# A two-block transformer on one core: residual, its projections and the norms turned from feature-major to token-major

## The chip, the core and the metric

The kernel runs on one core of a Trainium2 chip. TensorE (PE) multiplies; VectorE (DVE) and ScalarE (ACT) do elementwise work; GpSimd (POOL) does some; SyncE (SP) issues the DMAs. Every engine runs its own instruction stream in order, and semaphores order them among each other. The metric is the device time of one execution in microseconds.

## The reference

256 tokens of width 1024 pass through two blocks, everything in float32. Cut to what matters:

```python
def rmsnorm(x, g):
    return x * lax.rsqrt(jnp.mean(x * x, -1, keepdims=True) + EPS) * g

# block 1
u = rmsnorm(x, norm_mix_g);  p = u @ w_in + b_in          # q, kv, hq, hf, hi, hg, ga, gb
ya = window_attention(p) @ w_branch_attn;  yb = hgrn2(p) @ w_branch_hgrn
h = x + (sigmoid(ga) * ya + sigmoid(gb) * yb) @ w_out
u = rmsnorm(h, norm_ffn_g)
h = h + (silu(u @ w_ffn_gate) * (u @ w_ffn_up)) @ w_ffn_down      # hidden width 2816
x = rmsnorm(h, norm_final_g)
# block 2, modulated by a vector c
sh_m, sc_m, g_m, sh_f, sc_f, g_f = split(silu(c) @ w_ada + b_ada, 6)
h = rmsnorm(x, norm_mix_w) * (1 + sc_m) + sh_m
x = x + g_m * (concat(ssd(h @ w_in_2), chunk_attention(h @ w_in_2)) @ w_out_2)
h = rmsnorm(x, norm_ffn_w) * (1 + sc_f) + sh_f
x = x + g_f * (conv_ffn(h, w_up, w_down))
return rmsnorm(x, final_norm_w)
```

## The kernel before

All matrix products are float32 done as three fp32r products: a value is split into a high part (H) and a low remainder (L), and PE adds H·H, L·H and H·L. A weight matrix streams through in *panels* of four blocks of 128 rows by 512 columns (1 MB). SP loads a panel into one of 4 slots of `raw`; ACT writes its high part `wH` (L611, `split_hi`), DVE the remainder `wL` (L881 for the name `wL`, `split_lo`), both into one of 3 slots. The split of panel q+2 stands in the streams of ACT and DVE where PE starts panel q, so PE has two panels of cover. The operand of the products is `p1H`/`p1L`, `pyH`/`pyL` or `zH`/`zL`, [feature, k, token].

The order of all this is written out in `timeline()`: a list of events (panel, evac, tail, norm, ...), and every engine walks the same list and issues its own part of each event. Nothing is reordered.

Most groups (`GROUPS`, 512 output columns) are `cm`, feature-major: 128 weight columns are stationary and 256 tokens move (L1340, 128x256), four tiles to a group. `hi0`, `hi1`, `v2` and part of `kv` are `tm`, token-major: 128 tokens are stationary and the weight columns move (L1343, 128x512), two tiles to a group. The projections back to the residual are `out0`, `out1` (8 blocks each), `down0`, `down1` (22 blocks), `oo0`, `oo1` (8), `dd0`, `dd1` (22), all `cm`, and each tile is added on DVE to the residual `hT` [feature, k, token].

Norm n: 0 before `q0`, 1 before the gated FFN `f0`..`f10`, 2 before `xs`, 3 before `u0`, 4 at the end. ACT squares `hT` (L615), PE sums over the features by a matmul against `ones` (L1402; L1312 for norm 2), ACT takes the root (L634), DVE the reciprocal (L908), PE spreads it over the partitions (L1306), DVE scales (L884), ACT writes `p1H` (L642, L645), DVE `p1L`. At the start PE turns x with 16 transposes (L1302) while ACT squares the loaded rows.

The modulation `silu(c) @ w_ada` is a sum over rows on DVE: 24 panels of `w_ada` (event `ada`, four operations on `acc` each), and after every second one PE sums over the partitions (event `ada_sum`, L1438) and DVE reads the four columns into `mod`. `WITH_ADA` says with which weight panels they come: `q0`, `q1`, `ga1`, `out0`, `out1`, each `f`, and four each in `down0` and `down1`.

Of the kernel before, what the change touches and what calls it, by code (L numbers as in the profile page):

```python
# [5 lines left out]
F32 = mybir.dt.float32  # L6
# [7 lines left out]
P = 128  # L14
D = 1024
# [32 lines left out]
def tm_tiles(off, width):  # L48
    return [("tm", 2 + j, off, width, j) for j in range(TB)]
# [8 lines left out]
for _i in range(2):  # L58
# [5 lines left out]
    GROUPS[f"out{_i}"] = group("w_out", [(_i * W, W)], cm_tiles(4 - 4 * _i), "DDDD", "P1")  # L64
    GROUPS[f"down{_i}"] = group("w_ffn_down", [(_i * W, W)], cm_tiles(), "DDDD", "Z", KF)
    GROUPS[f"oo{_i}"] = group("w_out_2", [(_i * W, W)], cm_tiles(), "DDDD", "PY")
    GROUPS[f"dd{_i}"] = group("w_down_2", [(_i * W, W)], cm_tiles(4 - 4 * _i), "DDDD", "Z", KF)
# [16 lines left out]
WITH_ADA = [(_n, 1) for _n in ("q0", "q1")] + [("ga1", 0)]  # L84
WITH_ADA += [(_n, 0) for _n in ("out0", "out1")] + [(f"f{_i}", 0) for _i in range(NF)]
WITH_ADA += [(_n, _i) for _n in ("down0", "down1") for _i in range(4)]

# [5 lines left out]
def timeline():  # L93

    tl = [("load_x",), ("norm", 0), ("vectors",)]
# [3 lines left out]
    def gemm(name, *after):  # L99

        parts = len(GROUPS[name]["parts"])
        for i in range(parts):
# [3 lines left out]
            if (name, i) in WITH_ADA:  # L106
                j = next(ada)
                tl.append(("ada", j))
                if j % 2:
                    later.append(("ada_sum", j // 2))  # L110
# [4 lines left out]
            if i < len(after):  # L115
                tl.extend(after[i])

# [26 lines left out]
    gemm("out1", [("squares", 1)], [("norm", 1)])  # L144
    for i in range(NF):
        gemm(f"f{i}")
    gemm("down0")
    gemm("down1", [], [], [("squares", 2)], [("first_sums",)], [("mod",)], [("norm", 2)])
    assert next(ada, None) is None, "every panel of w_ada has its place"
    gemm("xs", [("h_final",)])  # L150
    gemm("bc", [("dt",)])
    gemm("q2", [], [("xdt",), ("sA", 0)])
# [4 lines left out]
    gemm("oo1", [("squares", 3)], [("norm", 3)])  # L157
    for i in range(NF):
        gemm(f"u{i}")
    gemm("dd0")  # L160
    gemm("dd1", [("gain",)], [("turn",)], [("squares", 4)], [], [], [("norm", 4), ("store",)])
# [3 lines left out]
def build(nc, IN, out):  # L165
# [17 lines left out]
    with ExitStack() as ctx:  # L183
# [8 lines left out]
        on.bcast = ctx.enter_context(nc.semaphore("bcast"))  # L192
# [69 lines left out]
        on.ot_done = ctx.enter_context(nc.semaphore("ot_done"))  # L262
        on.ot_psum = ctx.enter_context(nc.semaphore("ot_psum"))
# [12 lines left out]
        on.ms2_done = ctx.enter_context(nc.semaphore("ms2_done"))  # L276
        on.rt2_done = ctx.enter_context(nc.semaphore("rt2_done"))
        on.rd2_done = ctx.enter_context(nc.semaphore("rd2_done"))
# [28 lines left out]
        on.x_done = ctx.enter_context(nc.semaphore("x_done"))  # L307
        on.x_psum = ctx.enter_context(nc.semaphore("x_psum"))
# [3 lines left out]
        on.xr_zero = ctx.enter_context(nc.semaphore("xr_zero"))  # L312
        on.yT_done = ctx.enter_context(nc.semaphore("yT_done"))
# [48 lines left out]
        hT = sb("hT", [P, KD, T])  # L362
# [39 lines left out]
        OT, OUT = scr(28, KD, T), scr(8, TB, D)  # L402
# [1276 lines left out]
```

## Time and profile before

| | |
|---|---|
| time, median of 3 runs | 903.29 us (903.15 to 903.71) |
| span of the profiled execution | 902.7 us; the page gives no other time for it |
| PE busy | 859.8 us, 95% |
| DVE busy | 579.5 us, 64% |
| ACT busy | 474.3 us, 53% |
| POOL busy | 29.8 us, 3% |
| DMA queue q1 | 158.15 MB, 53.2% of 16 engines |
| mean granted clock of PE | 0.973 |

A row of the timeline is one instruction or a run of equal ones: start and duration in microseconds from the start of the span, engine, line of the kernel, operation, output<-inputs and shape, and in brackets how long the engine had been idle and what ended that. PE's durations overlap, since matmuls are pipelined: what a matmul costs a full PE is the distance to the next start, here called its pitch. PE's clock has two levels, granted 1.0 (2.4 GHz) and 0.5 (1.2 GHz).

### The profile page before, as it was taken

The numbers are of one execution on the slowest core, as the hardware profiler recorded it, in microseconds if no ns is written. First come the engines' busy times: TensorE is split into PE (matmuls) and PEld (weight loads), VectorE is DVE, ScalarE is ACT, GpSimd is POOL, SyncE is SP. The second block draws the span as 40 slices with busy tenths as digits, with TensorE's granted clock in tenths as the row PEclk, the third lists the DMA queues.
The fourth block names the chain that finished last, engine by engine and source line by source line (L and its number), as shares of the span: only waits on it lengthen the run. The fifth ranks groups of instructions, "written<-read, shape, count | busy, mean of one in ns | idle before, by whom it ended". The sixth has DMA issues, their size and how long they took to land. (4 is left out here: it accounts for less than half of the span.)

```text
span 902.7 us, 16064 instructions
## 1 busy us (share of the span) xinstructions
PE 859.8 (95%) x6874; PEld 841.7 (93%) x6874; DVE 579.5 (64%) x764; ACT 474.3 (53%) x687; POOL 29.8 (3%) x52
## 2 busy tenths in 40 slices
PE   5999999999899999999999999998989999999997
PEld 4999989999899989999999998997879999999997
DVE  5655457546646877777777767675444778777452
ACT  6656787637533444344333335735444666666342
POOL 3000001000100010000000000000001000000010
PEclk9999999999999989999999998999989999999999
DMA  9645344425442677888877864442424355654521
GB/s 315 237 154 189 124 140 141 154 81 187 143 138 79 206 229 245 267 258 260 266 256 274 278 230 174 153 141 63 144 66 149 97 184 187 187 187 164 188 71 47
DMA packets 105400, 159.18 MB, mean 176 GB/s; under 512 B 4320, under 2 KB 52720, under 8 KB 105328
## 3 DMA queue, kind: packets, MB, share of 16 engines
q1 hardware_dynamic: 105328, 158.15, 53.2%
q8 instruction: 54, 0.88, 0.4%
q14 instruction: 18, 0.15, 0.0%
HBM read 157.07 MB, written 1.06 MB: 175 GB/s over the span
## 5 line engine op out<-in xcount | busy, mean ns | idle before, releaser
L1340 PE MATMUL ps<-p1H,wH 128*128 128x256 f32 x1320 | 382.0, 289 | 10.6 <-DVE wL L881 4.6
L881 DVE TENSOR_TENSOR wL<-raw,wH 128x2048 fp32r<-128x2048 f32 (+1 forms) x126 | 282.4, 2243 | 154.6 <-ACT wH L611 154.0
L1340 PE MATMUL ps<-p1L,wH 128*128 128x256 f32 x1320 | 378.2, 286 | 0.0
L1340 PE MATMUL ps<-p1H,wL 128*128 128x256 f32 x1320 | 377.9, 286 | 0.0
L611 ACT ACTIVATE wH<-raw 128x2048 fp32r<-128x2048 f32 (+1 forms) x126 | 235.5, 1870 | 181.2 <-PE ps L1340 179.1
L1340 PEld LDWEIGHTS ps<-p1H,wH 128*128 128x128 f32 x1320 | 258.5, 196 | 12.0 <-DVE wL L881 4.9
L1340 PEld LDWEIGHTS ps<-p1L,wH 128*128 128x128 f32 x1320 | 258.6, 196 | 0.1
L1340 PEld LDWEIGHTS ps<-p1H,wL 128*128 128x128 f32 x1320 | 258.1, 196 | 0.0
L1340 PE MATMUL ps<-zH,wH 128*128 128x256 f32 x352 | 100.2, 285 | 2.2 <-DVE arena L881 1.1
L1340 PE MATMUL ps<-zL,wH 128*128 128x256 f32 x352 | 99.6, 283 | 0.0
L1340 PE MATMUL ps<-zH,wL 128*128 128x256 f32 x352 | 99.6, 283 | 0.0
L1340 PEld LDWEIGHTS ps<-zH,wH 128*128 128x128 f32 x352 | 67.5, 192 | 2.4 <-DVE wL L881 1.2
L1340 PEld LDWEIGHTS ps<-zL,wH 128*128 128x128 f32 x352 | 67.5, 192 | 0.0
L1340 PEld LDWEIGHTS ps<-zH,wL 128*128 128x128 f32 x352 | 67.5, 192 | 0.0
L884 DVE SCALAR_TENSOR_TENSOR acc<-raw,cact,acc 128x512 f32<-128x512 f32 x84 | 63.8, 759 | 2.6
L1340 PE MATMUL ps<-pyH,wH 128*128 128x256 f32 x192 | 55.8, 290 | 2.0 <-DVE pyL L881 1.2
L884 DVE SCALAR_TENSOR_TENSOR arena<-arena,par 128x256 f32<-128x256 f32 x120 | 50.0, 481 | 11.7 <-ACT arena L720 9.0
L1340 PE MATMUL ps<-pyL,wH 128*128 128x256 f32 x192 | 54.9, 286 | 0.0
L1340 PE MATMUL ps<-pyH,wL 128*128 128x256 f32 x192 | 54.8, 285 | 0.0
L659 ACT ACTIVATE arena<-ps 128x256 f32<-128x256 f32 x82 | 29.5, 377 | 26.7 <-PE ps L1340 26.3
L1340 PEld LDWEIGHTS ps<-pyH,wH 128*128 128x128 f32 x192 | 37.4, 195 | 2.7 <-issue 2.6
L1340 PEld LDWEIGHTS ps<-pyL,wH 128*128 128x128 f32 x192 | 37.5, 195 | 0.0
(247 smaller groups left out, 921.2 us busy)
## 6 DMA issues: line engine op xcount, KB each, us to landing
raw<-in_w_in SPq DMA_DIRECT2D x40, 1024.0 KB, 5.5
raw<-in_w_ada SPq DMA_DIRECT2D x24, 1024.0 KB, 5.2
raw<-in_w_up SPq DMA_DIRECT2D x44, 512.0 KB, 4.6
raw<-in_w_ffn_gate SPq DMA_DIRECT2D x22, 512.0 KB, 4.0
raw<-in_w_ffn_up SPq DMA_DIRECT2D x22, 512.0 KB, 5.4
raw<-in_w_ffn_down SPq DMA_DIRECT2D x10, 1024.0 KB, 5.5
raw<-in_w_down SPq DMA_DIRECT2D x10, 1024.0 KB, 5.0
raw<-in_w_out SPq DMA_DIRECT2D x8, 1024.0 KB, 5.1
```

What stands on the lines that cost most here:

```text
L611: nc.scalar.activation(wH[:, q % NHL, 0:nk, 0:wd], raw[:, i % NRAW, 0:nk, 0:wd], ACT.Copy).then_inc(on.w_hi, 1)
L659: nc.scalar.activation(dst(m), ps[:, t[1], 0:T], f, **bias).then_inc(on.evac_act, 1)
L881: return v.tensor_tensor(o, a, b, op)
L884: return v.scalar_tensor_tensor(out=o, in0=a, scalar=s, in1=b, op0=op0, op1=op1)
L1340: last = mm(ps[:, t[1], 0:T], wt[:, slot, k, t[2]:t[2] + P], at_[:, k0 + k, :], start=st, stop=en)
```

## The change

- The residual is `res` [token, feature], loaded straight into place; PE no longer turns x.
- `out`, `down`, `oo`, `dd` become `tm` groups of two tiles (j = 0, 1: the token halves), in other banks. In `group`, the odd two blocks of `down` and `dd` come first.
- The squares are summed by ACT itself (`accum_out`) over rows of 512; what the first half of the features gives is put together early (`before`). Root and reciprocal are taken for each token half (`root`, `turn_over`), and for j = 0 of `out1`, `oo1`, `dd1` inside the evacuation of the group, ahead of tile 1.
- The rows are scaled into `UN`, j = 0 by POOL (`scale`), j = 1 by DVE, 256 features at a time, and PE turns them back in four pieces of four transposes: two ahead of the first product, one after its block 1, one after block 2. ACT and DVE then write `p1H`, `p1L` from PSUM.
- The gates g_m and g_f are needed along rows: POOL writes a diagonal form `DG`, two float32 matmuls of 128x512 against `ones` spread it, ACT copies it (event `gate`, after the first panel of `q2` and of `u0`).
- The `ada` panels go to `ga0`, `hq0`, `hq1`, `hf1`, `bh0`, `out0` (2), `out1`, `f0`..`f9`, `down0` (5), `down1` (1), into buffers of their own, and PE's sums are gathered: 4 at norm 1, 2 at the end of `f10`, 4 at norm 2, 2 at norm 3.
- The final gain comes as a broadcast row by DMA; there are four output DMAs of 256 KB in place of two.

```diff
 def group(weights, segments, tiles, evac, operand, kblocks=KD, kbase=0):
-    parts = [(k, min(KP, kblocks - k)) for k in range(0, kblocks, KP)]
+    head = kblocks % KP
+    parts = [(0, head)] * (head > 0) + [(k, KP) for k in range(head, kblocks, KP)]
...
+    GROUPS[f"out{_i}"] = group("w_out", [(_i * W, W)], tm_tiles(0, W, 4 - 2 * _i), "DD", "P1")
+    GROUPS[f"down{_i}"] = group("w_ffn_down", [(_i * W, W)], tm_tiles(0, W, 4 - 2 * _i), "DD", "Z", KF)
+    GROUPS[f"oo{_i}"] = group("w_out_2", [(_i * W, W)], tm_tiles(0, W, 2 - 2 * _i), "DD", "PY")
+    GROUPS[f"dd{_i}"] = group("w_down_2", [(_i * W, W)], tm_tiles(0, W, 4 - 2 * _i), "DD", "Z", KF)
...
-WITH_ADA = [(_n, 1) for _n in ("q0", "q1")] + [("ga1", 0)]
...
+WITH_ADA = [(_n, 0) for _n in ("ga0", "hq0", "hq1", "hf1", "bh0", "out0")] + [("out0", 1), ("out1", 0)]
+WITH_ADA += [(f"f{_i}", 0) for _i in range(10)]
+WITH_ADA += [("down0", _i) for _i in range(1, 6)] + [("down1", 0)]
+
+ADA_READ = {1: (0, 4), "down0": (4, 2), 2: (6, 4), 3: (10, 2)}
...
-    gemm("oo1", [("squares", 3)], [("norm", 3)])
-    for i in range(NF):
+    gemm("oo1", [("squares", 3)], sums(3) + [("norm", 3)])
+    gemm("u0", [("gate", 1)])
+    for i in range(1, NF):
...
+            def scale(n):
+
+                pool.wait_ge(on.rd_done, 2 * n + 1)
+                for c in range(4):
+                    pool.tensor_scalar(UN[:, 0, wide(c)], (Y if n == 2 else res)[:, 0, wide(c)], R1[:, 0:1], None,
+                                       ALU.mult).then_inc(on.us0, 1)
...
+                elif e[0] == "gate":
+                    g = e[1]
+                    pool.wait_ge(on.ada_done, (2, 4)[g])
+                    pool.wait_ge(on.u_ready, (24, 32)[g])
...
+            def turn_over(n, j):
...
+                dve.wait_ge(on.rt_done, 2 * n + j + 1)
+                v.reciprocal(R1[:, j:j + 1], R0[:, j:j + 1]).then_inc(on.rd_done, 1)
...
+                        dve.wait_ge(on.tile_done, TILE[name, j])
+                        if n < 3:
+                            tt(hb, o, hb, ALU.add).then_inc(on.evac_dve, 1)
+                        else:
...
+                            step(tt(gt, o, gates[n - 3][:, half(i)], ALU.mult))
+                            tt(hb, gt, hb, ALU.add).then_inc(on.evac_dve, 1)
...
+                        if i == 1 and j == 0 and n != 2:
+                            turn_over(n, 0)
...
+            def turn(n, c):
+
+                pe.wait_ge(on.us0, 4 * n + c + 1)
+                pe.wait_ge(on.us1, 4 * n + c + 1)
+                if c > 1:
+                    pe.wait_ge(on.u_ready, 8 * n + 2 * c - 2)
+                for k in (2 * c, 2 * c + 1):
+                    for j in range(TB):
+                        last = tr(un(k)[:, j * P:(j + 1) * P], UN[:, j, k * P:(k + 1) * P])
+                last.then_inc(on.ut_psum, 1)
...
                     for k in range(nk):
                         pe.wait_ge(*operand_ready(name, k))
                         for t in g["tiles"]:
                             last = product(t, k)
+                        if name in NORM_OF and 0 < k < 3:
+                            turn(NORM_OF[name], k + 1)
```

The names below are those of the program: `arena` is the SBUF area that holds `UN`, `DG`, `TMP` and others, `R` the roots and reciprocals. ACT at the start of the program, before and then in the change (waits in brackets):

```order
L634 ACTIVATE R<-XSS,eps 128x2 [waits ss_done]
L611 ACTIVATE wH<-raw 128x2048 [waits raw0]
L642 ACTIVATE p1H<-arena 128x256 [waits tmp_done] x8
L611 ACTIVATE wH<-raw 128x2048 [waits raw1]
L752 ACT_TABLE_LOAD
```

```order
L679 ACTIVATE R<-XS,pre 128x1 [waits sq_done,pre_done]
L650 ACTIVATE wH<-raw 128x2048 [waits raw0]
L702 ACTIVATE p1H<-ps,par 128x256 [waits ut_psum] x8
L650 ACTIVATE wH<-raw 128x2048 [waits raw1]
L814 ACT_TABLE_LOAD
```

The high part of the second panel (raw1) still follows all eight `p1H`, which now wait for PE's transposes.

PE at norm 1, between the last product of `out1` and the first of `f0`, before and then in the change:

```order
L1340 MATMUL ps<-p1H,wL 128x256
L1402 MATMUL ps<-ones,arena 128x1 x10
L1306 MATMUL ps<-ident,R 128x128 x2
L1340 MATMUL ps<-p1H,wH 128x256
```

```order
L1431 MATMUL ps<-wL,p1H 128x512
L1489 MATMUL ps<-ones,acc 128x1 x8
L1489 MATMUL ps<-ones,arena 128x1 x8
L1396 MATMUL ps<-ident,arena 128x128 x8
L1428 MATMUL ps<-p1H,wH 128x256
```

The sums of squares and the spread are gone; four of the modulation's sums and eight transposes stand there.

POOL from norm 1 to norm 3, before and then in the change:

```order
L594 TENSOR_TENSOR arena<-arena 128x256 [waits sq_done]
L594 TENSOR_TENSOR arena<-arena 128x256 [waits sq_done,pool_step] x2
L588 MEMSET arena 128x2048 [waits u_ready]
```

```order
L574 TENSOR_SCALAR arena<-arena,R 128x256 [waits rd_done]
L574 TENSOR_SCALAR arena<-arena,R 128x256 x3
L629 MEMSET arena 128x2048 [waits h_final,u_ready]
L635 TENSOR_TENSOR arena<-ident,mod 128x1024 [waits u_ready,ada_done]
L574 TENSOR_SCALAR arena<-res,R 128x256 [waits rd_done]
L574 TENSOR_SCALAR arena<-res,R 128x256 x3
L635 TENSOR_TENSOR arena<-ident,mod 128x1024 [waits u_ready,ada_done]
```

L635 writes `DG`. The second one waits until all eight `p1L` of norm 3 stand (`u_ready`), and PE's spread of the gate stands behind the first panel of `u0`.

## Rows read from the trace of the kernel before

**Rows 1.** The chain that ended last: start us, us, what.

```profile
701.03 171.45 PE ps L1340 x1416
872.47 0.87 PE ps L1302 x8
```

**Rows 2.** Timeline of PE at the token-major group hi0 and what follows it.

```profile
215.60 0.40 PE L1343 MATMUL ps<-wH,p1H 128*128 128x512 f32 x1
...
226.51 0.28 PE L1340 MATMUL ps<-p1H,wH 128*128 128x256 f32 x1
```

**Rows 3.** Timeline, the last of twelve modulation sums on PE.

```profile
535.26 0.95 PE L1438 MATMUL ps<-ones,acc 128*128 128x1 f32 x8
...
536.07 0.36 PE L1340 MATMUL ps<-zH,wH 128*128 128x256 f32 x1
```

**Rows 4.** Timeline, banks that down0 and then down1 wait for.

```profile
469.03 0.36 PE L1340 MATMUL ps<-zH,wH 128*128 128x256 f32 x1 [1.15 <-DVE arena L881]
...
503.75 0.36 PE L1340 MATMUL ps<-zH,wH 128*128 128x256 f32 x1 [1.06 <-DVE hT L881]
```

**Rows 5.** Timeline of the start, PE, ACT and DVE.

```profile
16.51 0.58 PE L1340 MATMUL ps<-p1H,wH 128*128 128x256 f32 x1 [4.62 <-DVE wL L881]
...
19.38 1.90 ACT L611 ACTIVATE wH<-raw 128x2048 fp32r<-128x2048 f32 x1
...
25.84 3.70 ACT L611 ACTIVATE wH<-raw 128x2048 fp32r<-128x2048 f32 x2
...
27.77 4.49 DVE L881 TENSOR_TENSOR wL<-raw,wH 128x2048 fp32r<-128x2048 f32 x2 [4.17 <-ACT wH L611]
```

**Rows 6.** Timeline around norm 1.

```profile
324.88 2.29 DVE L881 TENSOR_TENSOR wL<-raw,wH 128x2048 fp32r<-128x2048 f32 x1 [0.29 <-ACT wH L611]
...
328.24 0.28 PE L1340 MATMUL ps<-p1H,wL 128*128 128x256 f32 x1
...
333.49 0.55 PE L1340 MATMUL ps<-p1H,wH 128*128 128x256 f32 x1 [1.57 <-DVE p1L L881]
```

**Rows 7.** Groups by line and shape: busy, mean ns | idle before, releaser.

```profile
L881 DVE TENSOR_TENSOR arena<-ps,brow 128x512 f32<-128x512 f32 x4 | 2.6, 680 | 0.0
L826 ACT ACTIVATE arena<-ps 128x512 f32<-128x512 f32 x4 | 2.4, 592 | 0.0
L1044 DVE TENSOR_SCALAR arena<-hT,par 128x256 f32<-128x256 f32 x8 | 2.4, 344 | 0.0
```

**Rows 8.** Timeline at norm 2 and norm 3.

```profile
538.90 0.28 PE L1340 MATMUL ps<-zH,wL 128*128 128x256 f32 x1
...
546.67 0.55 PE L1340 MATMUL ps<-p1H,wH 128*128 128x256 f32 x1 [0.87 <-DVE p1L L884]
...
695.63 0.28 PE L1340 MATMUL ps<-pyH,wL 128*128 128x256 f32 x1
...
698.08 0.26 ACT L634 ACTIVATE R<-ps,eps 128x2 f32<-128x2 f32 x1 [1.19 <-PE ps L1402]
...
701.03 0.55 PE L1340 MATMUL ps<-p1H,wH 128*128 128x256 f32 x1 [1.72 <-DVE p1L L884]
```

**Rows 9.** Stretch behind norm 3: length, busy PE, PEld, DVE, ACT, POOL, clock, DMA.

```profile
701.03:704.00 2.97, 2.97 (x14) 2.97 (x15) 2.97 (x9) 1.92 (x4) 0.00 (x0) 0.51 0.03 6
```

**Rows 10.** The chain: one float32 matmul of 128x256, in two instructions.

```profile
636.29 0.43 PE ps L1468 x2
```

**Rows 11.** Timeline, GpSimd.

```profile
8.63 0.37 POOL L564 TENSOR_SCALAR M<-CL 128x64 f32<-128x64 f32 x1
...
154.96 2.41 POOL L577 TENSOR_TENSOR arena<-arena 128x1024 f32<-128x1024 f32 x1 [143.32 <-ACT arena L810]
```

**Rows 12.** Instructions on acc: duration ns min/median/max.

```profile
L1098 DVE TENSOR_SCALAR acc<-raw,cact x12: 478/480/960, 32.2 to 522.2; 128x512 f32<-128x512 f32 x12
```

**Rows 13.** Timeline of the end.

```profile
893.22 0.28 PE L1340 MATMUL ps<-zH,wL 128*128 128x256 f32 x1
...
897.44 1.41 DVE L1076 TENSOR_SCALAR arena<-ps,R 128x512 f32<-128x512 f32 x2
```

More of the change, by code:

```diff
@@ L80 @@
 NU1 = 6
-WITH_ADA = [(_n, 1) for _n in ("q0", "q1")] + [("ga1", 0)]
-WITH_ADA += [(_n, 0) for _n in ("out0", "out1")] + [(f"f{_i}", 0) for _i in range(NF)]
-WITH_ADA += [(_n, _i) for _n in ("down0", "down1") for _i in range(4)]
+WITH_ADA = [(_n, 0) for _n in ("ga0", "hq0", "hq1", "hf1", "bh0", "out0")] + [("out0", 1), ("out1", 0)]
+WITH_ADA += [(f"f{_i}", 0) for _i in range(10)]
+WITH_ADA += [("down0", _i) for _i in range(1, 6)] + [("down1", 0)]
+ADA_READ = {1: (0, 4), "down0": (4, 2), 2: (6, 4), 3: (10, 2)}
+READS = list(ADA_READ)
+NORM_OF = {"q0": 0, "f0": 1, "xs": 2, "u0": 3}
+RES = {1: "out", 2: "down", 3: "oo", 4: "dd"}
 class Signals:
@@ L116, in gemm, with sums @@
                 tl.extend(after[i])
+    def sums(n):
+        q, count = ADA_READ[n]
+        return [("ada_sum", q + i, n) for i in range(count)]
     def X(u):
@@ L143, in timeline @@
     gemm("out0")
-    gemm("out1", [("squares", 1)], [("norm", 1)])
-    for i in range(NF):
+    gemm("out1", [("squares", 1)], sums(1) + [("norm", 1)])
+    for i in range(NF - 1):
         gemm(f"f{i}")
[L147 to L150, printed above, removed]
+    gemm(f"f{NF - 1}", [], sums("down0"))
+    gemm("down0", [("ada_read", "down0")])
+    gemm("down1", [], [], [("squares", 2)], [("mod", 0)], [], sums(2) + [("norm", 2)])
+    gemm("xs", [("h_final",), ("mod", 1)])
     gemm("bc", [("dt",)])
-    gemm("q2", [], [("xdt",), ("sA", 0)])
+    gemm("q2", [("gate", 0)], [("xdt",), ("sA", 0)])
     gemm("k2", [("sY", 0), ("sA", 1)], [("sY", 1), ("scores", 6)])
@@ L156, in timeline @@
     gemm("oo0", [("pt", 8), ("yT", 7), ("pv", 8), ("yT", 8)])
-    gemm("oo1", [("squares", 3)], [("norm", 3)])
-    for i in range(NF):
+    gemm("oo1", [("squares", 3)], sums(3) + [("norm", 3)])
+    gemm("u0", [("gate", 1)])
+    for i in range(1, NF):
         gemm(f"u{i}")
     gemm("dd0")
-    gemm("dd1", [("gain",)], [("turn",)], [("squares", 4)], [], [], [("norm", 4), ("store",)])
+    gemm("dd1", [], [], [("squares", 4)], [], [], [("norm", 4), ("store",)])
+    assert next(ada, None) is None, "every panel of w_ada has its place"
     return tl
@@ L633, in norm @@
-                sums = {0: XSS[:], 2: S12[:, :, 0], 4: ssf}.get(n, ss)
-                nc.scalar.activation(R0[:], sums, ACT.Sqrt, scale=1.0 / D, bias=eps[:, 0:1]).then_inc(on.rt_done, 1)
+                    for j in range(TB):
+                        square(0, 0, j)
+                for j in range(TB):
+                    square(n, 1, j)
+                    if n != 2:
+                        root(n, j)
                 if n == 4:
                     return
+                if n == 2:
+                    for j in range(TB):
+                        root(n, j)
@@ L761, in _ @@
                 elif k == "squares":
-                    for kk in range(4):
-                        square(e[1], kk)
+                    for j in range(TB):
+                        square(e[1], 0, j)
+                elif k == "gate":
+                    g = e[1]
+                    act.wait_ge(on.gate_psum, g + 1)
+                    if g == 0:
+                        act.wait_ge(on.conv_done, 24)
+                    for i in range(2):
+                        nc.scalar.activation(gates[g][:, half(i)], ps[:, 4 + i, :], ACT.Copy).then_inc(on.gate_done, 1)
                 elif k == "norm":
@@ L913, in norm @@
                     return
-                dve.wait_ge(on.bcast, n + 1)
+                dve.wait_ge(on.rd_done, 2 * n + 2)
+                for c in range(4):
+                    v.tensor_scalar(UN[:, 1, wide(c)], (Y if n == 2 else res)[:, 1, wide(c)], R1[:, 1:2], None,
+                                    ALU.mult).then_inc(on.us1, 1)
+                if n in ADA_READ:
+                    read_ada(n)
+                if n == 0:
+                    split_lo(0)
                 def low(k):
@@ L1437, in _ @@
                     for t in range(4):
[L1438 removed]
+                        o = 4 * (q - ADA_READ[n][0]) + t
+                        last = mm(adaps[n][:, o:o + 1], ACC[q][:, t * P:(t + 1) * P], ones[:, 0:1], start=True,
+                                  stop=True)
                     last.then_inc(on.ada_psum, 1)
[L1440 removed]
                 elif k == "scores":
```

450 lines of the change are left out of this document (211 added, 239 removed).

## The prediction, on record before the change was run

> **What bounds the kernel now.** I read the chain of waits first. From 701.03 PE issues 1416 matmuls of 128x256 in 171.45 us without a pause [rows 1]. That is most of block 2, and the page's 95% for PE says the same of the whole. So a microsecond is won where PE has less to issue, or where it stands still: at the start (first product at 16.51 [rows 5]), at norms 1, 2 and 3 (last product to next: 328.24 to 333.49 [rows 6]; 538.90 to 546.67 and 695.63 to 701.03 [rows 8]), at the end (893.22 to the span's 902.7 [rows 13]) and at two bank waits of 1.15 and 1.06 us [rows 4]. DVE and ACT have slack everywhere else. After a standstill comes a second cost: behind norm 3 the granted clock is 0.51, its lower level of 1.2 GHz, and 14 matmuls take 2.97 us [rows 9], 0.212 each against 0.120 for the others: (171.45 - 2.97) / 1402. Rows of the trace are taken against its span, 902.65 us; the median of the runs is 0.64 above it, and I add that at the end.
>
> **Wider products.** 48 matmuls of 128x512 run from 215.60 to 226.51 [rows 2], 0.2273 us each. Two of 128x256 cost 0.2404. The groups out, oo (64 products each), down, dd (176 each) make 480 x 3 = 1440 narrow matmuls, which become 720 wide ones: 720 x 0.0131 = **-9.4 us**. The pitch is that of the same form in the same kernel, so this term is firm.
>
> A rule speaks against it. The Trainium skill, "TensorE: Matmul & The Clock Gate", section "Wait — 56ns, not 53.3ns?", gives a full clock's pitch as columns / 2.4 GHz plus about 2.5 ns; by it halving the matmuls would save 2.5 ns for each of 720, an estimate of 1.8 us, and the sum would be 7.6 us higher. The rows show 13 ns, and they decide.
>
> **Modulation sums.** One lot (8 instructions on PE) stands between 535.26 and 536.07 [rows 3], 0.81 us, and there are 12 in line: 9.7 us. In the change ten of them stand in the waits of norms 1, 2 and 3, where PE has nothing else; the two behind f10 stay in line. Gain 10 x 0.81 = **-8.1 us**. If that cover were gone (the norms no longer wait), they would cost what they did. DVE's own part, about 3.1 us for each of 24 panels, only moves. In down0 and down1 it now stands in six panels in a row: 2.3 for a split and 3.1 together 5.4 us, against 24 x 0.227 = 5.45 on PE. PE's cover is two panels, so I take nothing and keep it as a rival. The sums of squares in down1 (16 instructions on PE, at 0.10 each as in [rows 3]) go: **-1.6 us**. The eight output transposes go from 872.47 [rows 1]: **-0.9 us**.
>
> **Bank waits.** Both [rows 4] end on DVE: down0 waits for the banks of f10, whose DVE step stood behind a read of the modulation; down1 waits for those of down0. In the change down0 writes banks 4, 5 and down1 banks 2, 3, and the read is behind: **-2.2 us**.
>
> **Norm 1.** Time is counted from the end of issue of the last product, E. DVE's split of the panel two ahead ends 327.17 (324.88 + 2.29), 1.2 us before E [rows 6], and about 0.9 before it now that the panel is shorter. Then in DVE's order: tile 0 (a 128x512 add with PSUM, 0.68 [rows 7]) to -0.2; ACT's square 0.59 plus the read of the accumulator, root 0.26 [rows 8], DVE's reciprocal, ready at +0.9. DVE has waited for it in `turn_over`, ahead of tile 1. Tile 1 to 1.6, square to 2.4, root and reciprocal to 2.95, first scaled piece to 3.3, all four by about 4.15. PE does four modulation sums to 3.3, the transposes from 3.4 (0.87 for eight [rows 1], more at the low clock), ACT's `p1H` to 4.8, DVE's `p1L` to 5.3. Before it was 5.13. With POOL in DVE's way (below) I take +0.5. Eight transposes more now stand inside the first panel: +0.9. Sum **+1.4**.
>
> **Norm 2.** Before 7.65. Now tile 0 and its gained copy `Y` to +0.5, tile 1 and its copy to 1.9, four squares on ACT to 2.65, two roots and two reciprocals one after the other to 3.95, four pieces to 5.1, TMP, `p1H`, `p1L` 1.4 more: 6.6. This is the norm where POOL's pieces fall on DVE's most; I take 7.85. With the transposes **+1.1**.
>
> **Norm 3.** Each tile now costs DVE two operations of 0.68 (gate, add). Tile 0 -0.95 to +0.45, its root and reciprocal to 1.7 with DVE waiting, tile 1 to 3.1, square, root, reciprocal to 4.4, pieces to 5.6, modulation read, TMP, `p1H`, `p1L` to 7.15, with POOL 7.5. Before 5.2: +2.3, transposes +0.9, **+3.2**. The clock's dip behind each norm I leave as it is.
>
> **The gates.** A float32 matmul of 128x256 takes 0.43 [rows 10], so one of 128x512 0.86; four of them in line **+3.4**. The first gate is ready long before. The second is not: POOL may write `DG` only when `p1L` 7 stands. With P the start of u0's first product: blocks 0 and 1 take to P+4.2 (2.97 us of it at the low clock), transposes to 4.6, block 2 to 6.05, transposes to 6.5, `p1L` 7 at 8.4, POOL's 128x1024 of 2.41 [rows 11] or more to about 11.2. PE has finished the panel at 7.95 and stands for **+3.3**. Another dip of the clock behind that is likely, 1.7 for a dip as long as at norm 3 (half of 3.4 us): **+1.7**.
>
> **The start.** Before: first product 16.51, high part of panel 1 from 19.38, then three table loads, high part of panel 2 from 25.84, its remainder done at 30.0; q1 began just then [rows 5]. The change frees DVE of the copies and lets the first product start near 15.3. But `p1H` 4 to 7 need transposes that stand behind blocks 1 and 2 of q0's first panel. At the low clock these blocks take until 20.4, so `p1H` 7 is ready at 23.7, and ACT's high part of panel 1 comes behind it: 23.7 to 25.6, remainder to 27.9, against a need at 24.3. The table loads follow: high part of panel 2 at 30.1, remainder 34.3, and q1 starts at 34.3 where it was 30.0, or at 35.4 if the clock dips in the standstill of 3.6. **+5.0**, between +4.2 and +6.
>
> **The end.** E to 902.7 is 9.3 us. In the change tile 1 runs to 1.6, root and reciprocal to 2.9, scaling to 4.0 where it was done 5.5 after E (897.44 + 1.41 [rows 13]); four DMA issues in place of two take back some: **-1.3**.
>
> **Sum.** -9.4 -8.1 -1.6 -0.9 -2.2 +1.4 +1.1 +3.2 +3.4 +3.3 +1.7 +5.0 -1.3 = -4.4: 898.3 of span, 898.9 as a median. POOL's scaling of 128x256 is in no row; it lies between 0.37 (64 columns) and 2.41 (two inputs, 1024) [rows 11]; I take 0.8.
>
> **Rivals.**
> - *The two new standstills don't come.* If the first products run at the full clock, or POOL's `DG` is done in time, the start (5.0) and the second gate (5.0) cost half or nothing: 891 to 895. For it: PE's order leaves one block's slack. Against it: the order of ACT and of POOL is fixed, and both chains are long. 894.
> - *DVE and POOL hold each other up.* An operation on `acc` of 0.48 us once took 0.96, while POOL was adding [rows 12]. If DVE's four pieces each wait for a piece of POOL's (0.8), norms 1 to 3 lose up to 1, 2.4 and 1, some 2.9 more than I took: 902. The Trainium skill, "SBUF — State Buffer", section "Who interferes with whom", says that DVE's `tensor_scalar` from SBUF to SBUF and a GpSimd operation exclude each other for a whole instruction; by that rule this rival is the forecast's neighbour, and the doubled duration agrees with it.
> - *Slower: DVE falls behind in down0.* Six panels at 5.4 us of DVE against 5.45 leave nothing for f10's tail (1.4) and down0's evacuation (4 x 0.68). And the loads are two of 1 MB in 5.45 us, 385 GB/s, over what q1 moves when it is full: 158.15 MB in 53.2% of 903 us, 329 GB/s. Twelve loads take 38 us where PE takes 30. It decides once the lag passes PE's cover, about 6.5 us; with 8 us of lag or DVE's and DMA's together, PE stands 4 to 8 us in down0 or down1, plus a clock dip: 906. Against it: four panels of `w_ada` in a row already ran here with no such wait in PE's list.
> - *The wide products save as little as the page's rule*: 906.
>
> **Chances.** Forecast 0.50, no standstills 0.17, DVE and POOL 0.14, slower 0.15, wide products 0.04. What a measurement of this kernel tells from no change is 0.2%, 1.8 us: faster means below 901.5, slower above 905.1. Faster: nine tenths of the forecast, the first rival, a third of the second: 0.66, which I cut to 0.64; slower: most of the last two, 0.17; between them 0.19. The range from 892 to 906 leaves out the lower end of the first rival and the upper end of the third.
>
> **What would show it.** Right: PE's pitch of 0.227 in out, down, oo and dd; no PE wait at the starts of down0 and down1; a standstill of 3 to 4 us ahead of q0's second panel, ended by `wL`; one of about 3 ahead of the gate's matmuls in u0, ended by POOL; gaps at norms 1, 2, 3 near 5.6, 7.9 and 7.5. Wrong: a PE wait on `wL` in down0 or down1; a dip of the clock that goes or comes where I left it; POOL's pieces far from 0.8.

## The result and the profile after

The changed kernel takes 909.92 us (median of 20 runs, 905.54 to 914.19), the kernel before 903.45 in as many. The ratio is 1.0064, 95% interval 1.0041 to 1.0086: slower by 0.6%, where 0.5% faster was forecast. The time lies above the forecast's range. The profiled execution has a span of 907.4 us, 4.7 more than the 902.7 of before; the forecast for it was 4.4 less.

The table sets the two traces side by side, stage by stage. A stage runs from the start of its first product to that of the next one's; the norms run from the end of issue of the last product to the first product, as in the prediction. The forecast's column puts its terms where they belong.

| stage | before | after | change | forecast |
|---|---|---|---|---|
| to the first product | 16.51 | 15.78 | -0.7 | -1.2 |
| q0 to attention | 35.22 | 40.58 | +5.4 | +5.4 |
| attention's first product to ba0 | 190.82 | 190.96 | +0.1 | 0 |
| ba0 to bh1 | 61.90 | 64.71 | +2.8 | 0 |
| out0, out1 | 23.91 | 21.79 | -2.1 | -2.1 |
| norm 1 | 5.13 | 8.64 | +3.5 | +0.5 |
| f0 to f10 | 135.54 | 131.83 | -3.7 | -3.5 |
| down0, down1 | 69.99 | 59.97 | -10.0 | -9.4 |
| norm 2 | 7.65 | 7.39 | -0.3 | +0.2 |
| block 2 up to oo0 | 118.25 | 123.62 | +5.4 | +2.6 |
| oo0, oo1 | 30.83 | 29.96 | -0.9 | -1.3 |
| norm 3 | 5.28 | 7.77 | +2.5 | +2.3 |
| u0 to u10 | 128.08 | 136.65 | +8.6 | +7.6 |
| dd0, dd1 | 64.23 | 59.87 | -4.4 | -4.4 |
| end | 9.36 | 7.88 | -1.5 | -1.3 |

Eleven of fifteen stages came within 0.6 us. Four carry the miss: ba0 to bh1 (2.8), norm 1 (3.0), block 2 (2.8) and u (1.0), together 9.6 us; span and forecast differ by 9.1, and the others give the rest back.

What was forecast as a new standstill is there. At the start, PE's timeline, then ACT's:

```profile
27.62 0.39 PE L1428 MATMUL ps<-p1H,wH 128*128 128x256 f32 x1 [3.63 <-DVE wL L950]
```

```profile
22.60 0.84 ACT L702 ACTIVATE p1H<-ps,par 128x256 fp32r<-128x256 f32 x2 [1.03 <-PE ps L1396]
23.32 1.91 ACT L650 ACTIVATE wH<-raw 128x2048 fp32r<-128x2048 f32 x1
25.25 1.28 ACT L814 ACT_TABLE_LOAD   x1
...
29.80 3.70 ACT L650 ACTIVATE wH<-raw 128x2048 fp32r<-128x2048 f32 x2
```

PE stands 3.63 us (forecast 3.6) for the split of panel 1, which ACT begins at 23.32, behind p1H 7 (forecast 23.7); the next split is at 29.80, where it was at 25.84 [rows 5]. In u0 PE stands for GpSimd's diagonals, as forecast (3.3), and then works at the low clock:

```profile
712.65 0.44 DVE p1L L950
713.20 1.94 POOLq L193
715.18 3.68 PE ps L1468 x4
```

These are pieces of the chain that ended last (start, us, what); PE's own row has [2.95 <-POOL arena L635] at 715.18.

**What was not forecast, first: DVE's order.** DVE's timeline ahead of bh1 and at norm 1:

```profile
294.80 0.48 DVE L1192 TENSOR_SCALAR arena<-raw,cact 128x512 f32<-128x512 f32 x1
295.32 2.33 DVE L953 SCALAR_TENSOR_TENSOR arena<-raw,cact,arena 128x512 f32<-128x512 f32 x3
297.68 2.29 DVE L950 TENSOR_TENSOR wL<-raw,wH 128x2048 fp32r<-128x2048 f32 x1
299.89 0.42 DVE L950 TENSOR_TENSOR arena<-ps,arena 128x256 f32<-128x256 f32 x1
...
330.08 3.11 DVE L953 SCALAR_TENSOR_TENSOR arena<-raw,cact,arena 128x512 f32<-128x512 f32 x4
333.23 0.17 DVE L972 TENSOR_SCALAR pre<-XS 128x2 f32<-128x2 f32 x1
333.30 2.28 DVE L950 TENSOR_TENSOR wL<-raw,wH 128x2048 fp32r<-128x2048 f32 x1
335.50 0.68 DVE L950 TENSOR_TENSOR res<-ps,res 128x512 f32<-128x512 f32 x1
337.36 0.16 DVE L981 RECIPROCAL R<-R 128x1 f32<-128x1 f32 x1 [1.18 <-ACT R L679]
337.44 0.67 DVE L950 TENSOR_TENSOR res<-ps,res 128x512 f32<-128x512 f32 x1
```

A panel of the modulation is read in 2.9 to 3.1 us. Before, none was read in the groups ba and bh. Now the panel that belongs to bh0 stands at 294.80, ahead of a split and of the evacuation of bh0's banks (299.89), and PE waits 1.59 us at 300.45, bh1's first product, for the first of these. At norm 1 the panel of out1 holds DVE until 333.19; the split ends at 335.58, 1.76 us after the end of PE's last product (333.82), where the forecast had it 0.9 ahead, and tile 0's add, which was to be done 0.2 ahead, starts at 335.50. Then tile 1's add waits for the root of tile 0, as forecast (337.36, 337.44). PE's own timeline at the two places:

```profile
300.45 0.36 PE L1428 MATMUL ps<-pyH,wH 128*128 128x256 f32 x1 [1.59 <-DVE arena L950]
...
335.52 2.83 PE L1489 MATMUL ps<-ones,arena 128*128 128x1 f32 x16
340.20 1.94 PE L1396 MATMUL ps<-ident,arena 128*128 128x128 f32 x8 [1.84 <-DVE arena L1000]
```

The four gathered sums end at 338.35 and PE then stands 1.84 us for DVE's scaled rows, so the sums themselves are not what makes norm 1 long.

**Second: the clock.** Windows of both traces (columns: us, length, then busy PE, PEld, DVE, ACT, POOL, the granted clock, DMA share, GB/s), before and after:

```profile
277.30:280.70 3.40, 2.94 (x14) 2.94 (x14) 0.20 (x1) 0.17 (x1) 0.00 (x0) 0.50 0.41 158
331.90:338.70 6.80, 5.23 (x25) 5.24 (x25) 5.99 (x16) 4.50 (x9) 0.00 (x0) 0.50 0.06 17
570.80:574.30 3.50, 3.50 (x18) 3.50 (x18) 1.05 (x6) 2.47 (x4) 0.00 (x0) 0.51 0.66 252
656.20:663.00 6.80, 6.25 (x23) 5.16 (x23) 3.16 (x9) 1.88 (x5) 0.00 (x0) 0.50 0.02 5
700.50:703.90 3.40, 2.87 (x13) 2.90 (x14) 3.40 (x9) 2.18 (x5) 0.00 (x0) 0.50 0.02 5
```

```profile
281.00:289.00 8.00, 6.66 (x34) 6.58 (x34) 3.67 (x6) 1.24 (x2) 0.00 (x0) 0.57 0.31 119
336.00:347.00 11.00, 8.83 (x44) 8.40 (x45) 4.85 (x13) 3.71 (x10) 3.66 (x4) 0.53 0.62 201
565.00:572.00 7.00, 7.00 (x35) 7.00 (x35) 3.60 (x8) 5.69 (x6) 0.00 (x0) 0.51 0.71 251
653.00:664.00 11.00, 9.38 (x34) 7.87 (x34) 4.64 (x14) 3.30 (x9) 0.00 (x0) 0.53 0.19 63
698.00:709.00 11.00, 7.94 (x38) 7.60 (x39) 5.21 (x15) 2.68 (x7) 2.90 (x3) 0.53 0.09 32
715.00:719.00 4.00, 3.82 (x7) 1.82 (x8) 2.27 (x1) 0.11 (x1) 0.12 (x1) 0.57 0.10 15
```

A window of 11 us at a mean of 0.53 holds 10.3 us at the low level of 1.2 GHz (11 x 0.47 / 0.5). So the low stretch at norm 1 grew from 6.8 to 10.3 us, that at norm 3 from 3.4 to 10.3, that at the y norm (653) from 6.8 to 10.3; those at 281 and 565 doubled, and those at 29 and 715 are new. Over the span the mean clock fell from 0.973 to 0.958: 902.7 x 0.027 / 0.5 = 49 us at the low level became 907.4 x 0.042 / 0.5 = 76. The forecast had added 3.4 for u0, and a dip at the start as a chance (q1 at 35.4 in place of 34.3).

Not all of the 27 us cost time. About 10 of them lie in the waits of the norms and at the end: the stretch at norm 1 runs from 336.3 to 346.6, the norm until 342.46, so that 4.1 us of it fall on f0, where it was 5.2 before (333.5 to 338.7). What costs is the low level where PE has products: by the ends of the stretches 3.4 us more at the start (29), 3.4 more at ba1 and bh0, 6 more in block 2, 6 more in u (5.4 behind norm 3 where it was 2.9, and 3.4 at 715). Block 2 as a whole, from the first product of xs to that of oo0, before and after:

```profile
546.67:664.92 118.25, 111.58 (x823) 105.57 (x823) 72.62 (x117) 62.73 (x102) 1.81 (x1) 0.94 0.40 134
```

```profile
541.65:665.27 123.62, 116.95 (x834) 109.68 (x835) 72.64 (x114) 63.47 (x105) 3.91 (x2) 0.92 0.39 128
```

In block 2 the narrow products of dt and those of the y norm fell into such stretches: from 561.2 to 567.8 where they took from 565.6 to 571.0 (1.2 us more), and from 654.07 to oo0 11.2 us instead of 9.7.

### The profile page after: what moved, and what is told of

It reads as the page before. It is cut to its first block and busy times, and to the rows that moved or that the text cites. A ratio compares the mean times of both kernels' runs of the same rounds, so it can differ in the third digit from the quotient of the medians.

```text
span 907.4 us, 14521 instructions
## 1 busy us (share of the span) xinstructions
PE 852.8 (94%) x6082; PEld 803.5 (89%) x6082; DVE 582.8 (64%) x742; ACT 479.0 (53%) x696; POOL 38.6 (4%) x60
## 5 line engine op out<-in xcount | busy, mean ns | idle before, releaser
L1431 PE MATMUL ps<-wH,zH 128*128 128x512 f32 x176 | 68.6, 390 | 0.0
L1431 PE MATMUL ps<-wL,zH 128*128 128x512 f32 x176 | 68.5, 389 | 0.0
L1431 PE MATMUL ps<-wH,zL 128*128 128x512 f32 x176 | 68.5, 389 | 0.0
L1396 PE MATMUL ps<-ident,arena 128*128 128x128 f32 x184 | 28.2, 300 | 16.4 <-DVE arena L1000 15.8
L953 DVE SCALAR_TENSOR_TENSOR arena<-raw,cact,arena 128x512 f32<-128x512 f32 x56 | 42.1, 751 | 1.7
L1428 PE MATMUL ps<-pyH,wH 128*128 128x256 f32 x128 | 37.3, 291 | 2.4 <-DVE arena L950 1.6
L1431 PEld LDWEIGHTS ps<-wL,zH 128*128 128x128 f32 x176 | 33.0, 188 | 6.9
L1431 PEld LDWEIGHTS ps<-wH,zH 128*128 128x128 f32 x176 | 33.0, 188 | 6.8
L1431 PEld LDWEIGHTS ps<-wH,zL 128*128 128x128 f32 x176 | 33.0, 188 | 6.8
L1396 PEld LDWEIGHTS ps<-ident,arena 128*128 128x128 f32 x184 | 23.5, 155 | 17.2 <-issue 9.8
```

Source lines behind the costliest of these rows:

```text
L953: return v.scalar_tensor_tensor(out=o, in0=a, scalar=s, in1=b, op0=op0, op1=op1)
L1396: return nc.tensor.transpose(o, i, ident[:])
L1428: last = mm(ps[:, t[1], 0:T], wt[:, slot, k, t[2]:t[2] + P], at_[:, k0 + k, :], start=st, stop=en)
L1431: last = mm(ps[:, t[1], 0:t[3]], at_[:, k0 + k, t[4] * P:(t[4] + 1) * P], wt[:, slot, k, t[2]:t[2] + t[3]], start=st, stop=en)
```

## Experiments

Each is the changed kernel with the edit shown, timed against the kernel before on the same chip. The changed kernel itself stands at 1.0064 (1.0041 to 1.0086). The ratios of e1, e3, e4 and e5 can't be told from that: what these edits do is read from the stages of one trace each, and "less than the changed kernel" compares medians of different sets of runs.

**e1: other places for the modulation's panels.**

```diff
-WITH_ADA = [(_n, 0) for _n in ("ga0", "hq0", "hq1", "hf1", "bh0", "out0")] + [("out0", 1), ("out1", 0)]
-WITH_ADA += [(f"f{_i}", 0) for _i in range(10)]
+WITH_ADA = [(_n, 0) for _n in ("ga0", "hq0", "hq1", "hf1", "bh0", "bh1")]
+WITH_ADA += [(f"f{_i}", 0) for _i in range(10)] + [("f3", 1), ("f6", 1)]
-ADA_READ = {1: (0, 4), "down0": (4, 2), 2: (6, 4), 3: (10, 2)}
+ADA_READ = {1: (0, 3), "down0": (3, 3), 2: (6, 4), 3: (10, 2)}
```

> Only the places of the modulation's panels change: the three that DVE read in the groups out0 and out1 go to bh1, f3 and f6, so three sums instead of four stand at norm 1 and three instead of two before down0. Theory (reads in the wrong place): in the changed kernel DVE's read of such a panel (about 2.9 us) stands ahead of the merge's adds and the product after bh1 waits 1.59 us for them, and another stands ahead of the split before norm 1, so that the residual's first add starts 1.7 us after PE's last product. Without them the 1.59 is gone and the gap of norm 1 (last product to first product, 8.6 us) falls to about 7.0: 3.2 us less, with 0 to 2 us more from shorter stretches at the low clock. Rival (GpSimd's scaling and DVE hold each other up at norm 1): the gap stays above 8.2, and only 1.6 us goes. Second rival (nothing gained, since the reads come back as waits in f3, f6 or down0): a PE wait on wL there of 1 us or more.

909.05 us, ratio 1.0075 (1.0057 to 1.0093). Norm 1 took 5.64 us instead of 8.64; the 3.0 are its whole miss:

```profile
336.00 0.68 DVE L950 TENSOR_TENSOR res<-ps,res 128x512 f32<-128x512 f32 x1
...
342.67 0.55 PE L1428 MATMUL ps<-p1H,wH 128*128 128x256 f32 x1 [0.32 <-DVE p1L L953]
```

DVE's add of tile 0 starts 1.03 us before the last product's end (337.03). So the read was the cause, and GpSimd's scaling, unchanged at 3.66 us, was not; the norm fell by 3.0 where 1.6 was expected. The other half of the expectation failed: PE still waits 1.79 us at 302.16. I had named the wrong panel; that of bh0 stood where it was. The total hardly moved, where 3.2 was expected: behind f10 stood three sums, the clock fell in down0 (61.38 us instead of 59.97), and the start took 1.2 us more at the low clock.

**e2: the start.** ACT's and DVE's split of panel 1 between p1H 3 and 4, the small vectors behind panel 0.

```diff
                 for k in range(KD):
+                    if n == 0 and k == 4:
+                        split_hi(1)
...
-    tl = [("norm", 0), ("vectors",)]
+    tl = [("norm", 0)]
-    gemm("q0", [], [("setup",)])
+    gemm("q0", [("vectors",)], [("setup",)])
```

> ACT splits panel 1 between p1H 3 and p1H 4, DVE likewise, and the three table loads with the small vectors come behind the split of panel 2. Theory (the start is late by ACT's order alone): the standstill of 3.63 us before q0's second panel goes to under 0.5, q1 starts at about 30 instead of 34.6, and the whole is 4 to 5 us faster, the clock aside. Rival (the loads of the first panels are what is late): a standstill of 2 us or more stays, ended by a load; gain under 2 us.

903.97 us, ratio 1.0012 (0.9988 to 1.0036), 6 us less than the changed kernel by the medians, 5 by the ratios. The standstill of 3.63 is gone, but q1 begins at 31.95, not at 30:

```profile
28.15 1.28 ACT L818 ACT_TABLE_LOAD   x1
...
31.36 1.55 ACT L721 ACTIVATE arena<-ps,par 128x256 f32<-128x256 f32 x4
```

The evacuation of q0's banks now stands behind the table loads, and PE waits 2.46 us for it. The timing theory holds, and its size (4 to 5) within the noise; the runs' mean clocks were 0.960 to 0.967 against 0.953 to 0.962 for the changed kernel.

**e3: a buffer of its own for the second gate's diagonals.**

```diff
-                    pool.wait_ge(on.u_ready, (24, 32)[g])
+                    if g == 0:
+                        pool.wait_ge(on.u_ready, 24)
-        ... DG = ..., scr(44, 8, P)
+        ... DG = ..., (scr(44, 8, P), scr(52, 8, P))
```

> The second gate's diagonals go to a buffer of their own (the place that Y had), so GpSimd needn't wait until the scaled tiles of norm 3 are used up. Theory: GpSimd writes them right behind its four scalings, by 704, the standstill of 2.95 us in u0 goes, and the stretch at the low clock behind it too: 3 us less, to 4.7 with the clock. Rival (GpSimd in DVE's way): its 2 us now fall on DVE's TMP and p1L steps of norm 3, whose first product comes 1 us or more later; 2 us less or fewer.

906.76 us, ratio 1.0056 (1.0038 to 1.0074): 3 us less by the medians, under 1 by the ratios. The standstill is gone; from u0's first product to dd0 131.45 us instead of 136.65. The rival holds in part: norm 3 took 8.55 us instead of 7.77, with GpSimd's 1.89 us from 705.54 over the first p1L, which took 1.22 instead of 0.43. e6 shows it more clearly. Block 2, which the edit does not touch, took 126.8 us in this trace instead of 123.6, with more of it at the low clock.

**e4: tile 1's add before tile 0's reciprocal.**

```diff
-                        if i == 1 and j == 0 and n != 2:
-                            turn_over(n, 0)
+                    if i == 1 and n != 2:
+                        turn_over(n, 0)
```

> At the end of out1, oo1 and dd1 DVE adds tile 1 before it takes the reciprocal of tile 0, where it stood for ACT's square and root of tile 0 (1.2 us) first. Theory (that wait is on the path that ends the norm): norm 1 and norm 3 each 1.2 us shorter (8.6 to 7.4; 7.8 to 6.6), the end 0.5 to 1.2: together 2.9 to 3.6 less. Rival (GpSimd's four pieces, now begun 0.2 to 0.7 later, become what the transposes wait for): norm 3 only 0.5 shorter or not at all; under 1.5 us in all.

908.72 us, ratio 1.0062 (1.004 to 1.0084). Norm 3 took 6.56 instead of 7.77 as expected, norm 1 7.73 instead of 8.64 (the split was late there anyhow), the end did not change at 7.88: what stands there is tile 1's own work. The total fell by 1.2 by the medians, and not at all by the ratios, less than the 2.1 in the norms and the 2.9 to 3.6 expected. In its trace two stages that the edit does not touch took 2.0 (q0 to attention) and 1.3 us (oo0, oo1) more, each with a low stretch of 6.8 us where the changed kernel has 3.4.

**e5: idle work on PE in the norms' waits.**

```diff
+            def fill(count, bank):
+                for _ in range(count):
+                    mm(ps[:, bank, 0:P], ident[:], ident[:], start=True, stop=True)
...
                     last.then_inc(on.ada_psum, 1)
+                    if n in (1, 2, 3):
+                        fill({1: 5, 2: 2, 3: 12}[n], 6)
```

> The changed kernel with idle work on PE in the waits of norms 1, 2 and 3: float32 products of the identity with itself (128x128, 0.11 us each by the transposes' pace) into a bank that nobody reads, 5, 2 and 12 behind each modulation sum and 6 behind the first transposes. Theory (the clock falls since PE stands or does next to nothing there): the stretches at the low clock behind the norms (336 to 347, 537 to 545 and 698 to 709 in the changed kernel, 10.2, 6.8 and 10.2 us long) become shorter by 3 us or more at two of the three, the norms' gaps keep their length (8.6, 7.4, 7.8), and the run is 2 to 6 us faster at a mean clock of 0.960 or more. Rival (the low stretches come from elsewhere, or at random): they stay as long; the time is the same or, by the filler in the way, 1 to 2 us longer.

909.04 us, ratio 1.0041 (1.0013 to 1.0069). The filler was twice as long as meant: 12 of them take 2.92 us by a row at 698.74, 0.24 each, and the row counts 24 instructions, two for each float32 product. Norms 1 to 3 grew to 10.2, 10.8 and 9.4. So the expected 2 to 6 us did not come, but the time did not grow either, for the clock stayed up behind two of them:

```profile
338.00:341.00 3.00, 3.00 (x29) 3.00 (x28) 2.19 (x6) 0.12 (x1) 2.15 (x3) 1.00 1.01 321
344.00:347.00 3.00, 3.00 (x28) 3.00 (x27) 0.06 (x1) 0.57 (x2) 0.00 (x0) 1.00 0.00 0
700.00:703.00 3.00, 3.00 (x29) 3.00 (x29) 1.37 (x5) 0.28 (x1) 0.04 (x1) 1.00 0.02 5
706.00:709.00 3.00, 3.00 (x29) 3.00 (x28) 1.67 (x4) 0.73 (x2) 0.00 (x0) 1.00 0.00 0
```

The same windows had 0.50 to 0.60 in the changed kernel. Its runs had clocks of 0.966 to 0.975. At norm 2, with a sum's four one-column products for each two fillers, the stretch of 6.8 us stayed, but it ended (543.1) before the longer norm did (543.60), and block 2 behind it was quicker:

```profile
543.60:664.46 120.86, 114.21 (x838) 107.10 (x836) 71.55 (x112) 62.94 (x104) 3.91 (x2) 0.94 0.40 131
```

That is 2.8 us less than in the changed kernel, for a norm that is 3.4 us longer. The low level behind norms 1 and 3 is the price of PE's standing still or doing one-column products there, and the rival (chance) is out.

**e6: the start, the buffer and the order of e2, e3 and e4 together**, with the table loads behind q0's evacuation and only four panels of the modulation read ahead of norm 1 (none in bh0).

```diff
+WITH_ADA = [(_n, 0) for _n in ("ga0", "hq0", "hq1", "hf1")]
+WITH_ADA += [(f"f{_i}", 0) for _i in range(10)] + [(f"f{_i}", 1) for _i in (1, 3, 5, 7)]
+ADA_READ = {1: (0, 2), "down0": (2, 4), 2: (6, 4), 3: (10, 2)}
+    gemm("q0", [], [("vectors",), ("setup",)])
```

> Together: the start's ACT order of e2 with the small vectors' table loads behind q0's evacuation, the buffer of e3, the order of e4, and four panels of the modulation, not eight, read ahead of norm 1 (that of bh0 too is gone; four more are read in f1, f3, f5, f7). Theory: the parts add up. Start: the 2.46 us standstill at q1 of e2 gone too, first product to the attention's first 35 to 36 us (40.6 in the changed kernel). Group bh: the wait of 1.6 us at its second half gone, since it was bh0's panel, which e1 had left in its place. Norm 1 under 5.2 (two sums, order), norm 3 6.6 to 7, no standstill in u0. Sum of gaps against the changed kernel: 3.6 + 2.5 + 1.6 + 3.5 + 1.2 + 2.9 = 15 less, so 893 to 896, faster than both kernels. Rival (what is saved comes back as low clock, or DVE falls behind in f and down0 with its fuller load): 899 or more.

898.09 us, ratio 0.9921 (0.9894 to 0.9948): faster than both, between theory and rival. Start 35.15 us, no wait at bh1's first product any more, norm 1 4.62, no standstill in u0. Two things took back the rest. Norm 3 was 8.05; GpSimd's and DVE's timelines there:

```profile
692.35 1.89 POOL L636 TENSOR_TENSOR arena<-ident,mod 128x1024 f32<-128x1024 f32 x1
```

```profile
691.59 0.98 DVE L1021 TENSOR_SCALAR arena<-ps,af,mod 128x256 f32<-128x256 f32 x2
692.60 1.93 DVE L951 TENSOR_TENSOR p1L<-arena,p1H 128x256 fp32r<-128x256 f32 x1
```

The p1L step (0.43 in e8) takes 1.93, and ends 0.29 after GpSimd's; the TMP steps, whose big input is in PSUM, are not held. The Trainium skill, "SBUF — State Buffer", section "Who interferes with whom", says just this: a DVE instruction with two SBUF inputs contends with a GpSimd instruction that reads SBUF. And the four sums of the late panels stood in a row behind f10, 16 one-column products in 32 instructions, with PE busy all the time:

```profile
458.68 4.08 PE L1492 MATMUL ps<-ones,arena 128*128 128x1 f32 x32
```

```profile
458.00:461.00 3.00, 3.00 (x30) 3.00 (x28) 0.54 (x2) 2.06 (x2) 0.00 (x0) 1.00 0.73 241
461.00:464.00 3.00, 3.00 (x15) 2.76 (x15) 2.86 (x3) 0.37 (x1) 0.00 (x0) 0.62 0.29 111
464.00:467.00 3.00, 3.00 (x8) 2.31 (x7) 0.00 (x0) 0.00 (x0) 0.00 (x0) 0.50 0.92 274
```

The rows put the fall at 461.7 (the window from 461 has 0.62), 3.0 us after the first of these products, while the last of them still ran; down0 and down1 took 62.72 us instead of 59.97.

**e7: e6 with e5's filler** (6, 2 and 8 behind each sum).

> e6 with the idle work of e5 (6, 2 and 8 behind each sum, 6 behind the transposes). Theory (standing still lowers the clock): another 2 to 5 us below e6, with shorter low stretches behind norms 1 to 3. Rival: equal to e6 or 1 to 2 us above it, where the filler is in the way of the shorter norm 1.

895.77 us, ratio 0.9893 (0.9853 to 0.9933). Norm 2 was 3.4 us longer and norm 1 2.0, and still it is not slower than e6: the stretch from norm 3 to dd0 fell from 132.00 to 129.35, and block 2 took 120.87 us instead of 122.78. The 2.3 us between the medians of e7 and e6 are within the noise of six and nine runs, so the total does not decide between theory and rival.

**e8: e6 with the sums spread and GpSimd's gate later.**

```diff
+    early = dict(zip((3, 4, 5, 7), sums("down0")))
+    for i in range(NF):
+        gemm(f"f{i}", [early[i]] if i in early else [])
...
+                    pool.wait_ge(on.u_ready, (24, 28)[g])
```

> e6 with two edits. The four modulation sums that stood behind f10 in a row stand one each in f3, f4, f5 and f7; and GpSimd writes the second gate's diagonals only when p1L 3 of u0 is there. Theory (a row of one-column products lets the clock fall as standing still does): in e6 the clock fell to 0.50 within 2.5 us of the start of the 32 products and stayed there 6.8 us; spread, it stays at 1.00 there, and down0 and down1 take 60.0 us instead of 62.7. Rival (that fall was chance, or came from the load on DVE): the clock falls at the start of down0 all the same. For norm 3: theory (GpSimd's 1.9 us held DVE's first p1L for 1.5 us) 8.05 to about 6.6; rival: stays near 8. Together 3 to 5 us below e6.

890.81 us, ratio 0.9832 (0.9772 to 0.9892). down0 and down1 take 59.87 us at a clock of 1.00; norm 3 6.56. Both theories hold, and both rivals fall. How many sums stood in a row behind f10 goes with what followed: two in the changed kernel, no low stretch in down0; three in e1, 3.4 us; four in e6, 6.8; none in e8, none. The total is 7.3 us below e6 by the medians (four runs against nine) and 5.1 by the profiled spans, where 3 to 5 was expected.

**e9: e8 with filler sized by e5's rows** (2 and 4 behind each sum, 3 and 4 behind the transposes, at norms 1 and 3).

> e8 with idle work sized by e5's rows (a float32 product of the identity takes 0.23 us, not 0.11): 2 behind each of the two sums and 3 behind the transposes at norm 1, 4 and 4 at norm 3, none at norm 2, where e5 and e7 showed the clock fall all the same. Theory: norms keep e8's length (4.6, 7.4, 6.6), the low stretches of 3.4 us behind norm 1 and of up to 10 us behind norm 3 go; 1.5 to 3 us below e8. Rival: equal, since a norm of 6.6 us alone no longer lowers the clock, or since so little filler is not enough.

890.37 us, ratio 0.9832 (0.9765 to 0.9899). Norms 1 to 3 take 4.62, 7.39 and 6.56 us, so the filler is hidden; behind norm 3 the clock stays up:

```profile
687.00:690.00 3.00, 2.95 (x26) 2.73 (x25) 2.49 (x8) 0.42 (x3) 3.00 (x4) 1.00 0.48 158
690.00:693.00 3.00, 2.18 (x19) 2.08 (x18) 2.35 (x6) 1.60 (x4) 0.16 (x1) 1.00 0.00 0
```

and from there to dd0 it takes 129.35 us instead of 131.15. Its spans are 887.9 to 889.5, those of e8 886.1 to 891.3, four runs each: in the total the two can't be told apart, so the expected 1.5 to 3 us are not shown. What the filler gave behind norms 1 and 3 (1.8 us in f, 1.8 in u) stands in this trace against 3.0 us more from q0 to ba0 and 1.0 from there to out0, where nothing was edited. At the norms themselves there is no doubt: e5, e7 and e9, the three traces with filler, are at 1.00 behind norms 1 and 3, and each of the eight others is at the low level there.

## Why the prediction was wrong

- **The direction failed by two steps, and both are of the kind "only moves".** They are worth 4.6 and 5.0 us of the 9.6 that the four missed stages carry; either alone brings the forecast's 898.3 of span to 903, no gain. The first: "DVE's own part, about 3.1 us for each of 24 panels, only moves", for which nothing was taken. The panels were looked at where six stand in a row, in down0, and there was no wait, as forecast. They cost where one stands ahead of something that PE waits for: 3.0 us at norm 1 (e1: 8.64 to 5.64) and 1.6 ahead of bh1 (gone in e6). The forecast took the row before norm 1 of the kernel before [rows 6], in which the split ended 1.2 us ahead of the last product, and didn't ask what the change puts in front of that split.
- **The second**: "The clock's dip behind each norm I leave as it is". It added 3.4 us at the low level for u0, where the span holds 27 more, of which some 17 fall on products. They cost 1.2 us in ba and bh (the 2.8 over forecast less the wait of 1.6), 2.8 in block 2 and 1.0 in u. Only the last stands behind a norm as the forecast meant it, and there its own figures should have warned it: norm 3 was to be 2.3 us longer, with less for PE to do in it. e5 and e9 show what the low level behind norms 1 and 3 depends on. The other 4.0 fall on products that the change left alone, and for which the forecast put nothing. In block 2 they go with the clock: e5 and e7, with about 14 us at the low level there, took 120.9 us, which is the forecast's figure (118.25 and 2.6), while e6, e8 and e9, with 18 to 19, took 122.8 to 123.2. e5 and e7 paid for it with a norm 2 that was 3.4 us longer, so no run gained it. At ba1 and bh0, with the same work for PE there, the stretch was absent in e2, 3.4 us in the kernel before, e1, e7 and e8 (ba0 to out0 61.93 us in e8), and 6.8 in the changed kernel and the rest (62.97 in e6). What sets its length there is open.
- **Sizes that held.** Wider products: 264 in 59.87 us, 0.2268 each (forecast 0.2273), and down, dd and out gained what was summed, so the rival on their saving is out. The rule that was weighed against it (the Trainium skill, "TensorE: Matmul & The Clock Gate", section "Wait — 56ns, not 53.3ns?") gave 2.5 ns for each merged pair; the rows give 13.6 (2 x 0.1202 less 0.2268). Sums out of line, squares, output transposes, bank waits and norms 2 and 3: each within 0.6.
- **The start** was right in mechanism and size (3.63 us, ended by the split; q1 begins at 34.95 where it was 30.20, 4.75 later against +5.0), and e2 shows that it was ACT's order. The second gate likewise: 2.95 against 3.3, and e3 removes it. The gates' products were forecast at 1.7 each: the first took 1.71 (581.19 to the second product behind it, 583.02, less its 0.12), the second 3.51 (715.18 to 718.81, likewise) in the low stretch behind the standstill.
- **The rivals.** "Standstills don't come" is out. "DVE and POOL hold each other up" did not happen in the norms of the changed kernel, where DVE's four pieces took 1.65 to 1.94 beside GpSimd's 3.7 to 3.9 (0.92 to 1.12 a piece, taken as 0.8), against 1.4 by [rows 7]: 0.3 to 0.5 more, not a piece of GpSimd's for each; it did in e3 and e6, on another pair of instructions. "DVE falls behind in down0" did not happen, though its time, 906, was nearest. It was the right engine in the wrong place.
- The change can pay: e8, which keeps all of it and mends order and places, is 1.7% faster than the kernel before (0.9772 to 0.9892). No run gives the kernel before the same places for the panels, the sums and the table loads, so how much of the 1.7% is the change's own is not shown.

## What to carry to other kernels

When a change moves work on an engine with slack, list for each moved piece what now stands behind it on that engine and which of these PE waits for; slack on average says nothing about the last 3 us before a norm. Work that is gathered into a wait is free only if the clock is the same afterwards: idle time and rows of one-column products belong in the sum twice, once as themselves and once as the low stretch that may follow them. The low stretches are to be counted over the whole kernel: here 4.0 of the 5.0 us that they cost fell where the change did nothing. And mend what the trace shows before giving a change up: of the small edits only that of the start was clear of the noise alone (5 to 6 us), yet together they turned 0.6% slower into 0.8% faster, and two more into 1.7%.

## What the runs showed of the hardware

- 16 one-column float32 products in a row (32 instructions, 4.08 us, PE busy throughout) were followed by 6.8 us at the low clock in the middle of dense work (e6); spread one lot at a time they were not (e8). A PE that the profile shows busy can still fall to the low clock.
- The clock differs between runs of one kernel: that of before had spans from 897.8 us at a mean of 0.979 to 911.9 at 0.961. A profile of one run can't show the typical clock; the stages' lengths at the full level can be compared, the total less so.
- A float32 product of 128x128 takes 0.24 us, twice a transpose of that shape (0.11 by [rows 1]).
- At the full clock a product of the weights took 0.1202 us with 256 columns and 0.2268 with 512. Both are 13.5 ns more than the columns divided by 2.4 GHz, so in these rows the extra is paid once for each product, whatever its width, and merging two saves it once.
